# Reordering the set-up of the first Strassen pair, and accumulating one LayerNorm mean on TensorE

## The reference

```
x = LN(alpha*x + 0.5 * (silu(x @ wg0) * (x @ wu0)) @ wd0)        # first feed-forward, 2816 hidden
q,k,v,b,c,h = split(x @ w_in)
x = LN(alpha*x + concat(attention(q,k,v), b * conv3(c*h)) @ w_out)
x = LN(alpha*x + 0.5 * (silu(x @ wg1) * (x @ wu1)) @ wd1)        # second feed-forward
```

## Time and profile before

| | |
|---|---|
| median of 3 runs | 1042.13 us (1041.46 to 1044.23) |
| the profiled execution: its time, its span | 1044.41 us, 1042.6 us |
| PE busy in the span | 994.1 us (95%) |
| DVE, ACT, POOL busy | 690.8, 467.2, 69.6 us |
| mean granted TensorE clock | 0.982 |

### The profile page before, as it was taken

One profiled execution on the slowest core, in us unless ns is written; L12 is line 12 of the kernel. 1 busy time (PEld: TensorE's weight loads), 2 busy tenths in 40 slices (PEclk: granted clock), 3 DMA queues, 4 the chain that ended last, 5 costly groups with the idle time before them and its releaser, 6 DMA issues. The chain is left out here.

```text
span 1042.6 us, 18161 instructions
## 1 busy us (share of the span) xinstructions
PE 994.1 (95%) x7526; PEld 970.7 (93%) x7526; DVE 690.8 (66%) x990; ACT 467.2 (45%) x780; POOL 69.6 (7%) x80
## 2 busy tenths in 40 slices
PE   8979999999999999999999989679999999999994
PEld 7979999999999999999988988679999999999994
DVE  5887843577886468626666687787743587784457
ACT  4445531245445235545556456444521344553230
POOL 2000000000000000016142000000000000000004
PEclk9989999999999999999999999889999999999998
DMA  9463343133225333452113461033342222336402
GB/s 254 98 119 107 110 133 102 31 90 125 81 82 173 97 116 81 106 182 82 42 42 94 136 209 57 20 110 103 115 119 62 82 81 82 95 103 194 151 1 86
DMA packets 131594, 108.19 MB, mean 104 GB/s; under 512 B 13138, under 2 KB 129590, under 8 KB 131496
## 3 DMA queue, kind: packets, MB, share of 16 engines
q1 hardware_dynamic: 130368, 105.46, 34.1%
q10 hardware_dynamic: 1144, 1.57, 1.3%
HBM read 103.08 MB, written 4.95 MB: 104 GB/s over the span
## 5 line engine op out<-in xcount | busy, mean ns | idle before, releaser
L1056 PE MATMUL banks<-h_hi,w_hi 128*128 128x280 f32 (+1 forms) x480 | 139.1, 290 | 0.0
L1056 PE MATMUL banks<-h_hi,w_lo 128*128 128x280 f32 (+1 forms) x480 | 139.0, 289 | 0.0
L1056 PE MATMUL banks<-h_lo,w_hi 128*128 128x280 f32 (+1 forms) x480 | 138.8, 289 | 0.0
L877 PE MATMUL banks<-x_hi,w_hi 128*128 128x280 f32 (+1 forms) x416 | 126.3, 304 | 3.1 <-DVE x_lo L2127 0.9
L1043 PE MATMUL banks<-x_hi,w_hi 128*128 128x280 f32 (+1 forms) x400 | 118.5, 296 | 9.3 <-ACT ln_sq L1452 7.4
L877 PE MATMUL banks<-x_lo,w_hi 128*128 128x280 f32 (+1 forms) x416 | 120.8, 290 | 0.0
L877 PE MATMUL banks<-x_hi,w_lo 128*128 128x280 f32 (+1 forms) x416 | 120.7, 290 | 0.0
L1043 PE MATMUL banks<-x_hi,w_lo 128*128 128x280 f32 (+1 forms) x400 | 117.5, 294 | 0.0
L1043 PE MATMUL banks<-x_lo,w_hi 128*128 128x280 f32 (+1 forms) x400 | 117.3, 293 | 0.0
L1762 DVE TENSOR_TENSOR w_lo<-w_raw,w_hi 128x1024 fp32r<-128x1024 f32 (+1 forms) x66 | 77.9, 1182 | 56.6 <-ACT w_hi L1350 56.6
L1043 PE MATMUL banks<-t_hi,w_hi 128*128 128x280 f32 x336 | 99.7, 297 | 9.8 <-ACT silu_g L1442 8.8
(11 more groups left out here) (236 smaller groups left out, 2660.0 us busy)
## 6 DMA issues: line engine op xcount, KB each, us to landing
w_raw<-in_ffn_w_down SPq DMA_DIRECT2D x30, 512.0 KB, 4.0
more_raw<-in_ffn_w_down SPq DMA_DIRECT2D x28, 512.0 KB, 3.6
w_raw<-in_ffn_w_gate SPq DMA_DIRECT2D x24, 512.0 KB, 4.0
w_raw<-in_ffn_w_up SPq DMA_DIRECT2D x24, 512.0 KB, 4.7
more_raw<-in_ffn_w_gate SPq DMA_DIRECT2D x20, 512.0 KB, 4.1
more_raw<-in_ffn_w_up SPq DMA_DIRECT2D x20, 512.0 KB, 5.5
w_raw<-in_w_in SPq DMA_DIRECT2D x14, 512.0 KB, 4.6
w_raw<-in_w_out SPq DMA_DIRECT2D x32, 128.0 KB, 3.0
```

Of the source, the lines that this page charges most:

```text
L877: mm = nc.tensor.matmul(out[:, 0:n], w[:, t, :], x(k), start=(k == ends[0] and w is hi and x is rhs_hi), stop=(k == ends[1] and w is lo))
L1056: mm = nc.tensor.matmul(out, w[:, k - k0, c * P:(c + 1) * P], h[:, k, cols(half, f)], start=(k == 0 and w is hi and h is h_hi), stop=(ku = ...
```

## The change

It does the following.

- `ln_mean_part`: for L = 3, TensorE multiplies each of the 8 residual chunks by the matrix of 1/1024 and accumulates in a bank of its own (`mean_bank(3)` is `aux[3]`). Chunks 0 to 5 come in steps k = 10 to 15 of the output projection, 6 and 7 between the first direct products. VectorE's running sum for L = 3 is gone.
- For f = 1, VectorE does the lo part of product 0 before `ln_center(3)` and block sum 0 behind `ln_sum_squares(3)`; ScalarE copies hi of products 0 and 1 before `ln_square(3)`. The wait for the mixer's output transfers moves ahead of them.
- In `gate_up_first`, block sums, combinations, hi copies and lo parts stand in a new order, and `bias_residual(3)` is in two parts, of which the first is enough for combination 0.
- For f = 0, `parameters()` is later on VectorE (behind the lo part of product 3), and the table's transfer is the last thing of ScalarE's list.
- The semaphore counts are fitted to the new order.

```diff
...
         def width(half, late=0):
             return cols(half, late).stop - cols(half, late).start
+        def mean_bank(L):
+            return aux[3] if L == 3 else aux[0]
...
         def ln_cols(L):
...
                     pe.wait_ge(centered, KT * L)
-                nc.tensor.matmul(aux[0][:, 0:ln_width(L)], mean_of[:, :], ln_sum[:, half, 0:ln_width(L)], start=True, stop=False)
-                nc.tensor.matmul(aux[0][:, 0:ln_width(L)], mean_of[:, :], x_res[:, KT - 1, ln_cols(L)],
+                nc.tensor.matmul(mean_bank(L)[:, 0:ln_width(L)], mean_of[:, :], ln_sum[:, half, 0:ln_width(L)], start=True, stop=False)
+                nc.tensor.matmul(mean_bank(L)[:, 0:ln_width(L)], mean_of[:, :], x_res[:, KT - 1, ln_cols(L)],
                                  start=False, stop=True).then_inc(mean_done, 1)
...
+            def ln_mean_part(L, c):
...
+                pe.wait_ge(r_done, r_count(L, c))
+                mm = nc.tensor.matmul(mean_bank(L)[:, 0:ln_width(L)], mean_of[:, :], x_res[:, c, ln_cols(L)],
+                                      start=c == 0, stop=c == KT - 1)
+                if c == KT - 1:
+                    mm.then_inc(mean_done, 1)
             def ln_var(L):
...
                             mm = products(acc[v], n, range(k, k + 1), *x_operands(0, f), t0=k)
+                            if (v, k) == (0, 1):
+                                ln_mean_part(3, KT - 2)
                             if (v, k) == (0, 3):
-                                ln_mean(3)
+                                ln_mean_part(3, KT - 1)
                             if (v, k) == (2, 2):
...
                         pe.wait_ge(pt_copied, 2 * len(ITEMS))
+                        pe.wait_ge(centered, 4 * KT)
                     else:
...
                     ln_var(2)
+                if k >= 10:
+                    ln_mean_part(3, k - 10)
                 products(acc[wo_bank(k)], n, range(2, KT), *mix, t0=2).then_inc(steps_done, 1)
...
                 hidden_hi(f, 0, 1)
-                next_hi(n)
-                next_hi(n + 1)
-                if f:
-                    bias_residual(3, range(KT))
-                    silu(f, 1, 0)
-                    combination_hi(f, 1)
-                else:
+                if f == 0:
+                    next_hi(n)
+                    next_hi(n + 1)
                     combination_hi(f, 1)
                     silu(f, 1, 0)
-                combination_hi(f, 0)
+                    combination_hi(f, 0)
+                    next_hi(n + 2)
+                else:
+                    bias_residual(3, range(0, QT))
+                    silu(f, 1, 0)
+                    bias_residual(3, range(QT, KT))
+                    next_hi(n + 2)
+                    combination_hi(f, 1)
+                    combination_hi(f, 0)
+                hidden_hi(f, 1, 0)
+                silu(f, 1, 1)
+                next_hi(n + 3)
+                product_copy(f, 0, 0)
+                hidden_hi(f, 1, 1)
+                combination_hi(f, 2)
+                next_hi(n + 4)
+                next_hi(n + 5)
+                product_copy(f, 0, 2)
+                combination_hi(f, 3)
                 if f == 0:
...
                     act.dma_start(bias_dram, bias_row[:, :].unsqueeze(1).to_broadcast([N_HEADS, QMAX, T_W])).then_inc(bias_out, 16)
-                next_hi(n + 2)
-                hidden_hi(f, 1, 0)
-                next_hi(n + 3)
-                silu(f, 1, 1)
-                product_copy(f, 0, 0)
-                combination_hi(f, 2)
-                hidden_hi(f, 1, 1)
-                next_hi(n + 4)
-                product_copy(f, 0, 2)
-                combination_hi(f, 3)
-                next_hi(n + 5)
             def product_copy(f, j, s):
...
             def feed_forward(f):
                 if f == 1:
+                    act.wait_ge(outputs_out, 16 * MIXER_OUTS)
+                    next_hi(U_GU[1] + 4)
+                    next_hi(U_GU[1] + 5)
                     ln_square(3)
...
                     ln_hi(3, range(4, KT))
-                    act.wait_ge(outputs_out, 16 * MIXER_OUTS)
                 gate_up_first(f, ahead=f + 1)
...
                 _, f, j, s = UNITS[n]
-                if s == 2:
+                if s == 2 and j:
                     block_sum(f, j, 2)
...
                 block_lo(f, j, s)
-                if s == 1:
+                if s == 1 and j:
                     block_sum(f, j, 0)
-                if s == (2 if j == 0 else 1):
                     block_sum(f, j, 1)
             def hidden(f, half, ab, first=False):
...
                 b21, b22 = x_res[:, QT:KT, 0:HALF], x_res[:, QT:KT, HALF:TOK]
-                if f and i == 0:
-                    dve.wait_ge(res_biased, 4 * KT)
+                if f and i < 2:
+                    dve.wait_ge(res_biased, 3 * KT + (QT if i == 0 else KT))
                 if i in (1, 3):
...
                 hidden_lo(f, 0, 1)
-                next_lo(n)
-                if f:
+                if f == 0:
+                    next_lo(n)
+                    next_lo(n + 1)
+                    block_sum(f, 0, 0)
+                    combination(f, 0)
+                    combination(f, 1)
+                    combination_lo(f, 1)
+                    block_sum(f, 0, 2)
                     hidden(f, 1, 0)
-                next_lo(n + 1)
-                combination(f, 0)
-                combination(f, 1)
-                if f == 0:
+                    block_sum(f, 0, 3)
+                else:
+                    block_sum(f, 0, 2)
+                    combination(f, 0)
                     hidden(f, 1, 0)
-                combination_lo(f, 1)
+                    combination(f, 1)
+                    next_lo(n + 1)
+                    combination_lo(f, 1)
+                    block_sum(f, 0, 3)
+                next_lo(n + 2)
+                combination_lo(f, 0)
+                block_sum(f, 0, 1)
+                hidden(f, 1, 1)
+                next_lo(n + 3)
                 if f == 0:
                     parameters()
-                next_lo(n + 2)
                 hidden_lo(f, 1, 0)
-                combination_lo(f, 0)
-                next_lo(n + 3)
-                hidden(f, 1, 1)
                 combination(f, 2)
...
                 combination(f, 3)
+                next_lo(n + 5)
                 hidden_lo(f, 1, 1)
-                next_lo(n + 5)
                 combination_lo(f, 3)
             def pair_step(f, j, s):
...
                     nc.vector.tensor_tensor(x, x, a, ALU.add).then_inc(r_done, 1)
-                if last or L >= 4 or first:
+                if last or L >= 3 or first:
                     return
...
                     x = x_res[:, c, ln_cols(L)]
-                    nc.vector.tensor_tensor(x, x, aux[0][:, 0:ln_width(L)], ALU.subtract).then_inc(centered, 1)
+                    nc.vector.tensor_tensor(x, x, mean_bank(L)[:, 0:ln_width(L)], ALU.subtract).then_inc(centered, 1)
             def ln_sum_squares(L):
...
             def feed_forward(f):
                 if f == 1:
+                    dve.wait_ge(outputs_out, 16 * MIXER_OUTS)
+                    next_lo(U_GU[1] + 4)
                     ln_center(3)
                     ln_sum_squares(3)
+                    block_sum(f, 0, 0)
                     ln_rstd(3)
...
                     ln_apply(3, range(4, KT))
-                    dve.wait_ge(outputs_out, 16 * MIXER_OUTS)
                 gate_up_first(f, ahead=f + 1)
...
```

## The result

The changed kernel takes 1034.57 us (median of 6 runs, 1032.17 to 1036.71), the kernel before 1042.07 on the same chip (6 runs, 1041.46 to 1044.23). The ratio is 0.9925, with a 95% interval of 0.9907 to 0.9943: 7.5 us faster. That is inside the range (1028.2 to 1036.5), but 3.9 us above the 1030.7 that was predicted and outside the forecast's own range (1028.5 to 1033.5). The sum promised 11.4 us.

The account below looks back on a forecast made before the run. The prediction took pair 0's setup in both feed-forwards, mainly VectorE's list up to L1888, plus a slow clock, as the bound. 9.0 + 1.2 + 1.2 = 11.4 us off 1042.13 gave about 1030.7 us, range 1028.2 to 1036.5.

Parts of the forecast that it names:

- The sum: Whole kernel: 9.0 for FF1's list, 1.2 for the clock and 1.2 for FF0 make 11.4 us.
- FF1, the list: Second feed-forward, pair 0: reordered lists bring VectorE's first add L1888 earlier, gain 9.0 us (7.4 to 11.0).
- the walk's own check: FF1's list: counting removed VectorE work and waits against new waits gives 7.8 to 8.6 us.
- The walk's waits: Pair 0 of FF1, lists followed instruction by instruction: 0.8 us new waits, 1.2 behind combination 2, 0.3 for product 2.
- FF1, the front: Layer norm of L = 3: the mean's 1.9 us gain is spent on moved splits; nothing gained up to the last lo part.
- the second rival: FF1's front slips or the clock doesn't stay up after the 3.0 us idle before the variance: 1032.9 us, 15%.
- The clock: FF1's pair 1 runs at full clock after the shorter wait before product 6: gain 1.2 us (0 to 1.2).
- FF0: First feed-forward, pair 0: lists only reordered, L1888 earlier, gain 1.2 us (loss of 2.6 to gain of 1.7).
- The first rival: Issuing the table's transfer holds ScalarE 5.08 us instead of 1.27; FF0's L1888 3.8 us later: 1034.5 us, 12%.
- The table's transfer: Moved to about 60 to 90 us, beside loads of pairs 2 and 3; its effect on them stays hidden, no cost.
- the last rival: The table's write starves loads of pairs 2 and 3: 1042.0 us (3%), or 1045.3 and more (4%).

Follow-up runs that it names:

- e7: The kernel before with only the bias table's sum and transfer moved to their late places: 1046.55 us, ratio 1.0031.
- e1: The changed kernel run again unchanged: 1035.23 us, ratio 0.9917.
- e2: The changed kernel with the first feed-forward's old ScalarE and VectorE lists, and the table's sum and transfer, put back: 1034.29 us, ratio 0.9918.
- e4: The changed kernel with TensorE's variance matmuls of L = 3 seven steps later among the direct products: 1034.98 us, ratio 0.9922.
- e5: The changed kernel with the table's sum and transfer back in their old early place, new block lists kept: 1032.69 us, ratio 0.9901.
- e6: The changed kernel with the table's transfer issued only in the first feed-forward's first down part (170.58 us): 1033.06 us, ratio 0.99.
- e11: The kernel before with only the mean of L = 3 moved to TensorE, all lists as before: 1041.77 us, ratio 0.9991.
- e9: e6 with the second feed-forward's two early hi copies moved behind the squares and its lo part behind the sum of squares: 1030.14 us, ratio 0.9884.
- e3: The changed kernel with VectorE's running sum and the old mean of L = 3 put back, new lists kept: 1038.74 us, ratio 0.9954.
- e10: e9 with 16 dummy matmuls in TensorE's wait ahead of product 5 of the first pair, both feed-forwards: 1033.35 us, ratio 0.9912.
- e8: The changed kernel with the second feed-forward's old lists put back, mean on TensorE and first feed-forward's new lists kept: 1040.04 us, ratio 0.9969.

## Why the prediction was right, and where it was off

**FF1, the list (predicted 9.0 with the front at nothing): right, 9.3 between the two profiles.** From the reciprocal to the first add it is 44.73 us before and 35.39 to 35.41 in seven of the nine traces that have the new list (35.61 and 35.77 in the others). The other traces with the old list have 43.72 to 44.26, so 8.3 to 9.3 is the fair size, and the walk's own check (7.8 to 8.6) was as good as its 9.0. Part of what a front gains or loses comes back in the list behind it (e7's front is 1.3 us longer than before's and its list 1.0 shorter), so the two together are the steadier measure: 75.4 and 75.7 us in before and e7, 67.0 to 68.6 in the changed kernel, e1, e2, e4, e5 and e6, that is 6.8 to 8.7 us less. The walk's waits are there one by one: [0.77] in front of product 3's lo part where 0.8 was put, and [1.21] behind combination 2; product 2 waits 0.67 us where 0.3 was put.

**FF1, the front ("up to the last lo part of L = 3 nothing is gained"): failed.** The front grew from 30.71 to 32.85 us in the first profile, 32.15 in e1: 1.4 to 2.1 us lost. Three things were off. Without the running sum VectorE starts the next instruction of a step 0.54 us after the residual (e11, above) and not 0.36, so a step saves 0.30 us and not 0.48. The 0.36 was read behind the addition to the running sum; behind a residual the next start came 0.47 us later in the earlier trace rows too. By itself the mean brings centering forward by 1.15 us and the reciprocal by 1.6, not 1.9. Second, the splits don't spend just that: they hold centering up by 2.5 us (24.1 us after the reciprocal of L = 2 with them, 21.6 without: e6 and e9). ScalarE finishes its biases, then two hi copies, and VectorE waits 1.42 us for the first of them. The walk put centering 0.5 us late; it came 1.4 us late. Third, PE's 3.04 us wait for the variance was forecast, and that the clock could fall there was the second rival: in the first profile, e5 and e6 it fell, in e1 and e2 it didn't. e9 shows that none of it had to be: the moved work fits behind the squares.

**The clock (predicted 1.2): right in size, measured 1.5.** FF1's pair 1 ran at full clock in all traces with the new list but e3's, which has the old mean, and e10's, where the longer idle was put in. The 0.3 us more has a plain reason: the prediction took FF0's pair as the full-clock yardstick (22.06), and FF1's, with 264 columns in half 0, takes 21.77. The reason given, that a slow product 5 leaves only about 1.5 us in front of product 6, is not what the first profile shows. There product 6 waited 2.48 us, longer than the 2.29 of before, and ran at full clock all the same. In e1, e2, e4, e5, e6 and e9 the wait was short, 1.20 to 1.73. So the result agreed, in the first profile not for that reason, and what decides it stays open. Nor is it a property of the new list alone: of the four traces with the old one, pair 1 was slow in two (before and e11) and at full clock in two (e7 and e8, after waits of 2.43 and 2.39 us). So on an average of executions the term is nearer half its size.

**FF0 (predicted 1.2): right, measured 1.5.** e2 gives it back in its trace. The first rival, an issue of 5 us, did not come: the transfer's issue took 1.28 us.

```profile
55.31 1.28 ACTq L1447 DMA_DIRECT2D bias_dram<-bias_row  x1
```

**The table's transfer ("Hidden"): failed, and it is the largest miss.** e7 shows it alone: 3.3 us. The step that failed is the landing time of pair 2's loads. The walk gave each load the time of its own 512 KB at 54 GB/s, 10 us, and let the last of the four land at 72, wanted at 88. In e1 the four were issued at 55.1, 57.4, 57.8 and 60.4 and landed 3.6, 22.3, 30.0 and 29.4 us later, the last at 89.8. They were wanted at about 86, and in the first profile, where they landed 3.8, 13.2, 20.9 and 26.5 us after their issue, at about 85.

One thing that the walk left out is that the four stand in one queue, SP's. At 54 GB/s their 2.1 MB take 39 us, which from 55 is 94: nearer than 72, but 4 us later than e1's last landing and, from 54, 7 us later than the first profile's. It isn't the whole mechanism either. This is what e1's DMA queues (q10 has the write, q1 SP's loads) moved from 55 to 82.5 us:

```profile
q10 hardware_dynamic: 808, 1.23, 38.0%
q1 hardware_dynamic: 2286, 2.28, 27.1%
```

SP's queue had then moved more than the 2.1 MB of the four loads, and two of the four were still out, for 5 and 7 us more; bytes of pair 3's loads, issued from 75.1, must have gone ahead of their last ones. The write's last packets are between 88 and 89 us, so the last load landed about 1 us behind it. In before all four landed just behind the write, whose last packets are before 75: at 75.5, 76.9, 78.3 and 79.6. But the second load of e1 landed at 79.7, in the middle of the write, and all four of the first profile before its end. So the last rival had the place right (pair 2's weights, this transfer) and its effect too large: it put the last landing at 97, 7 us behind the write, and the time at 1042.0. What holds up the last parts of a load beside this write no run separates. The rule of the Trainium skill, "DMA: Bandwidth & Descriptors", Queues, rings and completion order, that an engine goes round its queue rows packet by packet, agrees with the loads that landed while the write ran; the prediction's conclusion from it, that the sum then stands, does not follow and was wrong.

Put together, the sum with these sizes: 9.3 - 1.4 to 2.1 for the front, 1.5 for FF0, 1.5 for the clock, and -2.9 for the wait on the loads (e1's pair 1 against 22.0) make 7.3 to 8.0 us, against the 7.5 measured. It is not exact: the clock term is some 0.7 less on an average of executions, front and list together are 6.8 to 8.7, and the wait costs nothing in two of the six traces that have the transfer late, 2.9 in e1, and 3.1 to 3.2 with 1.4 to 1.5 for the clock behind it in three. The first profile, in which the loads were just in time and the start was 1.7 us shorter, hid that: its 12.2 us agreed with the prediction by luck. What stays open is why the landing varies between 23.7 and 30.0 us from one execution to the next, and how often.

## What to carry to other kernels

To say when a load lands beside another transfer, do not count its own bytes alone: what stands ahead of it in its queue counts too, and even that sum was 4 to 7 us off here, so compare with the end of the other transfer as well. Move a large background transfer only into a stretch in which no load has a due time. Work that is pulled ahead of a chain to fill a hole must lie in the hole: behind the step whose result others wait for, not in front of it. Before idle time of TensorE is filled, ask which wait the filling makes longer: a slow clock in front of a wait is free, and one behind it is not.

## What the runs showed of the hardware

The clock after a pause is not the same in each execution. The 3.04 us wait in front of L923 was followed by matmuls at the lower level (1.27 us a pair) in the first profile, e5 and e6, and at the full one (0.71 us) in e1 and e2; 2.28 or 2.29 us in front of product 6 brought it down in e5 (FF0) and in before, e3 and e11 (FF1), and 2.38 to 2.53 us did not in e1, e3 (FF0), e7, e8 and the first profile. So the length of the pause alone does not decide it. A kernel with many pauses of 2 to 4 us therefore has several possible times, a microsecond or two apart, and one profile shows one of them.
